# A two-layer hybrid convolution trunk on eight cores: trimmed halo, loads in another order, first groups by halves with filler matmuls, last LayerNorms by halves

## The chip, the cores and the metric

The kernel runs on the 8 cores of one Trainium2 chip. Each core computes 2048 tokens of its own, and no core waits for another. The metric is the device time of the slowest core in microseconds (us), as the median of several runs.

## What is computed

The reference runs two layers (DEPTH = 2) over x of shape (2, 8192, 1024) in float32. Each layer has one input projection, three causal mixers side by side, one output projection and a LayerNorm over the sum with the input:

```python
def hybrid_layer(x, ...):
    h = einsum("btd,de->bte", x, w_in)                       # 1024 -> 4608
    a_bg, a_cg, a_v, a_z, b_v, b_g, b_z, c_u, c_z = split(h) # 9 parts of 512
    y_a = a_bg * conv3(a_cg * a_v) * silu(a_z)               # A: short conv
    u_b = silu(layer_norm(conv31(b_v * sigmoid(b_g))))       # B: conv over 31
    y_b = u_b * silu(b_z)
    p = trailing_mean(c_u, windows 2, 4, 8, 16) - c_u        # C: pooling
    y_c = (p @ pool_w + pool_b) * pool_scale * silu(c_z)
    out = concat(y_a, y_b, y_c) @ w_out                      # 1536 -> 1024
    return layer_norm(ALPHA * x + out, ln_g, ln_b)
```

A token needs earlier tokens: 2 in mixer A, 30 in mixer B and 15 in mixer C, in each layer.

## The kernel before

**Tokens.** A core holds its 2048 tokens and 64 before them, the halo (`HALO = 64`, `TOK = 2112`). The halo is computed again on each core, so that no core needs another's first layer. The work is cut into four units (`UNITS`, L475 and after): layer 0 block 0, layer 0 block 1, layer 1 block 0, layer 1 block 1. `unit_tiles` cuts a unit into tiles of tokens: in block 0 three tiles, (0, 320), (320, 384), (704, 384) in layer 0 and (32, 288), (320, 384), (704, 384) in layer 1; in block 1 two tiles of 512. The later tiles get what lies before them from small tail buffers.

**Groups.** The input projection is computed with channels on the partitions. `group` (L509) makes one 128-channel output of one tile: 8 matmuls (L523) that add up over the 1024 inputs into one PSUM bank, with as many columns as the tile has tokens. Steps are made of groups: `B_step` has three (value `v`, gate `g`, `z`), `A_step` four (`v`, `cg`, `z`, `bg`), `C_step` two (`u`, `z`). Each kind has four channel groups, so a unit has 36 groups per tile. `unit_order` puts them in order: in unit 0 B0, A0, B1, B2, B3, A1, A2, A3, C0 to C3; in the others all B, all A, all C.

**Mixer B.** Inside `B_step`, `glu` makes the gated values (ScalarE, then VectorE) and issues four small DMAs from SBUF to SBUF on SyncE's queue (L640, in the trace `mem<-mem`), which lay out shifted copies. `conv` (L670) then runs 32 matmuls with 32 output columns of the array each, four side by side; they need `Lm`, which VectorE makes by `emit_diag` (L576) from `dmask` and `w4`. `lnb` and `gate` finish mixer B.

**Loads.** Weights of the input projection (`wrg`, 256 KB on the chip each, one per group) go through a ring of `NSLOT = 9` buffers: `issue_w(k + 9)` follows the last tile that used slot k. They, the transposed input `xT` (five tiles, L497) and `wo` (L491) are issued on GpSimd's queue. The inputs of the residual (`Rb`, five buffers), `lnbc`, `par`, `w4` and the `mem<-mem` copies go through SyncE's queue. At the start GpSimd issues w0, xT tile 0 in two halves of its contraction, w1, w2, xT tile 1, w3, xT tile 2, w4 to w8; SyncE issues six small loads at once.

**Output projection.** `p2_chunk` (L976) takes 128 tokens: twice 12 matmuls of 512 columns, then on VectorE residual and statistics (`res`), a square root on ScalarE, and the scaling. The chunks of a unit are mixed into the B groups of the next one (`p2fill`); those of the last unit come at the end. There all but the last chunk are scaled on ScalarE (L549), multiplied on GpSimd (L553) and shifted on VectorE (L553); the last one is scaled and shifted by halves on VectorE (L558) and stored by halves (L1002).

**Order.** All of it is recorded by `P.add` in program order per engine. A planner (`Clock`, with costs and landing times per instruction) decides at build time where the pieces of the side work stand; `spawn(t, ...)` places something at the planner's time t. A `Res` is the unit of dependence: an `Rb` buffer has one for all of its 1024 columns.

## Time and profile before

| | us |
|---|---|
| median of 3 runs (839.61 to 840.76) | 840.51 |
| the profiled execution | 837.62 |
| its span on the slowest core (core 6) | 836.1 |
| spans of the eight cores | 827.0 to 836.1 |
| TensorE busy (matmuls) | 791.8 |
| VectorE, ScalarE, GpSimd busy | 535.5, 399.7, 298.0 |

The profile is one execution, seen on its slowest core. Busy time of PE is modelled (a matmul's row is longer than the distance to the next one), so the distance from start to start is the better measure of a matmul. PEclk is the TensorE clock that was granted, as a share of 2.4 GHz. The KB of a DMA are those that arrive in SBUF (bf16); in memory weights and xT are float32.

### The profile page before, as it was taken

The page shows a single profiled execution, that of the slowest core. Times are in us where ns is not written, and L with a number is a line of the kernel's source. Part 1 is how long each engine was busy: PE and PEld are TensorE (multiplying, and loading weights), DVE is VectorE, ACT ScalarE, POOL GpSimd, SP SyncE. Part 2 cuts the span into 40 slices and gives each one's busy share as a digit, 9 for nine tenths or more (in the row PEclk, how much of TensorE's full clock was granted, in tenths as well). Part 3 has the DMA queues.
Part 4 walks back from the last instruction along what each step waited for, and adds up shares of the span by engine and source line. Part 5 has one row for each costly group of instructions (what it writes and reads, how often), then busy time and mean ns, then how long its engine had stood idle before and what let it go on. Part 6 is the DMA issues. An engine that isn't in the chain of part 4 may idle for free.

```text
span 836.1 us, 16279 instructions; the slowest of 8 cores (827.0 to 836.1 us)
## 1 busy us (share of the span) xinstructions
PE 791.8 (95%) x5208; PEld 408.6 (49%) x5208; DVE 535.5 (64%) x816; ACT 399.7 (48%) x648; POOL 298.0 (36%) x374
## 2 busy tenths in 40 slices
PE   2999889999999999999999999999999999999993
PEld 1555446654444444445555556666444444444441
DVE  1332148887656568668665567868765565888686
ACT  0222257445646487334555578534543348544421
POOL 3122117737110016336510125653711113772342
PEclk9899989999999999999999999999999999999997
DMA  8969996752565755555555676894266756341042
GB/s 127 204 102 206 164 211 98 114 82 42 143 161 141 188 131 92 86 76 77 128 121 158 172 173 146 139 148 66 39 169 169 189 135 152 58 55 35 1 176 102
DMA packets 59170, 104.01 MB, mean 124 GB/s; under 512 B 7216, under 2 KB 28208, under 8 KB 58576
## 3 DMA queue, kind: packets, MB, share of 16 engines
q0 software_dynamic: 28944, 61.26, 43.4%
q1 hardware_dynamic: 30144, 41.72, 16.7%
q8 instruction: 44, 0.72, 0.4%
q14 instruction: 38, 0.31, 0.1%
HBM read 116.52 MB, written 16.78 MB: 159 GB/s over the span
## 4 chain that ended last, share of the span: by engine, by line
PE 78%; DMA 8%; DVE 8%; issue 3%; SPq 1%; ACT 1%; POOL 0%; DVEq 0%; ACTq 0%; POOLq 0%
PE ps L523 49%; PE ps L976 20%; PE ps L670 7%; DMA mem<-mem 6%; DVE mem L553 5%; DMA xT<-xint 2%; DVE mem L558 2%; PE pT L1060 1%; ACT mem L549 1%; SPq L640 1%; PE ps L700 1%; PE ps L714 1%; PE ps L901 1%; DVE Rb L558 1%; DMA out<-Rb 0%
## 5 line engine op out<-in xcount | busy, mean ns | idle before, releaser
L523 PE MATMUL ps<-xT,wrg 128*128 128x512 bf16 (+3 forms) x2880 | 541.7, 344 | 18.4 <-DMA xT<-xint 15.6
L523 PEld LDWEIGHTS ps<-xT,wrg 128*128 128x128 bf16 x2880 | 279.3, 99 | 258.4 <-issue 38.9
L549 ACT ACTIVATE mem<-ps 128x512 f32<-128x512 f32 (+8 forms) x284 | 132.0, 487 | 148.5 <-PE ps L523 115.1
L976 PE MATMUL ps<-wo,yb 128*128 128x512 bf16 (+1 forms) x792 | 184.3, 379 | 0.5 <-ACT mem L549 0.5
L553 POOL TENSOR_TENSOR yb<-mem 128x512 bf16<-128x512 f32 (+3 forms) x120 | 129.1, 1082 | 137.0 <-ACT mem L549 81.7
L487 POOL DMA_DIRECT2D wrg<-w_in_r x144 | 80.0, 559 | 241.0 <-PE ps L523 154.3
L549 ACT ACT_TABLE_LOAD x72 | 92.4, 1283 | 80.6 <-DVE mv L1011 49.6
L976 PEld LDWEIGHTS ps<-wo,yb 128*128 128x128 bf16 (+1 forms) x792 | 77.2, 98 | 90.7 <-issue 3.2
L553 DVE TENSOR_TENSOR mem<-mem 128x512 f32<-128x512 f32 (+11 forms) x140 | 108.9, 784 | 15.7 <-POOL mem L553 4.0
L549 ACT ACTIVATE mem<-mem,par 128x384 f32<-128x384 f32 (+3 forms) x80 | 57.7, 734 | 87.0 <-DVE mem L553 74.5
L558 DVE SCALAR_TENSOR_TENSOR Rb<-Rb,ps 128x512 f32<-128x512 f32 (+1 forms) x66 | 45.1, 684 | 72.6 <-PE ps L976 72.3
L558 DVE SCALAR_TENSOR_TENSOR mem<-mem,par 128x384 f32<-128x384 f32 (+3 forms) x80 | 67.7, 846 | 15.1 <-ACT mem L549 10.0
L670 PE MATMUL ps<-mem,Lm 128*32 128x384 bf16 (+3 forms) x1280 | 69.2, 349 | 8.1 <-DMA mem<-mem 7.9
L553 DVE TENSOR_TENSOR mem<-ps,mem 128x512 f32<-128x512 f32 (+3 forms) x80 | 46.2, 585 | 42.9 <-PE ps L523 24.8
L558 DVE SCALAR_TENSOR_TENSOR Rb<-Rb,mv,lnbc_s 128x1024 f32<-128x1024 f32 (+2 forms) x54 | 67.9, 1258 | 8.1 <-DMA out<-Rb 2.4
L558 DVE SCALAR_TENSOR_TENSOR mem<-mem,ps 128x384 bf16<-128x384 f32 (+3 forms) x40 | 23.4, 585 | 67.6 <-ACT mem L549 67.6
L670 PEld LDWEIGHTS ps<-mem,Lm 128*32 128x32 bf16 x1280 | 32.9, 98 | 41.8 <-issue 24.4
L990 DVE BATCH_NORM_STATS2 stt<-Rb 128x6 f32<-128x512 f32 (+1 forms) x66 | 45.8, 694 | 6.8
L549 ACT ACTIVATE mem<-ps,par 128x384 bf16<-128x384 f32 (+3 forms) x40 | 24.3, 608 | 51.0 <-PE ps L670 51.0
L553 POOL TENSOR_TENSOR mem<-mem 128x384 f32<-128x384 bf16 (+3 forms) x40 | 42.5, 1072 | 0.3
L558 DVE SCALAR_TENSOR_TENSOR mem<-mem 128x384 bf16<-128x384 f32 (+3 forms) x40 | 34.1, 854 | 6.1 <-DVE mem L553 3.3
L1051 POOL DMA_DIRECT2D x1s<-Rb x16 | 8.7, 542 | 78.5 <-DVE Rb L558 78.5
(48 smaller groups left out, 329.4 us busy)
## 6 DMA issues: line engine op xcount, KB each, us to landing
wrg<-w_in_r POOLq DMA_DIRECT2D x144, 256.0 KB, 5.2
mem<-mem SPq DMA_DIRECT2D x64, 135.0 KB, 3.2
Rb<-xin SPq DMA_DIRECT2D x16, 512.0 KB, 5.3
x1s<-Rb POOLq DMA_DIRECT2D x16, 512.0 KB, 3.8
Rb<-x1s SPq DMA_DIRECT2D x16, 512.0 KB, 4.6
mem<-mem SPq DMA_DIRECT2D x64, 103.0 KB, 5.7
wo<-w_out_r POOLq DMA_DIRECT2D x24, 256.0 KB, 7.4
out<-Rb POOLq DMA_DIRECT2D x8, 512.0 KB, 4.0
```

What stands on the lines that cost most here:

```text
L487: P.add("pool", lambda e: e.dma_start(out=wrg_t[:, k % NSLOT].rearrange("p k c -> p (k c)"), in_=w_in_d[li, ci]), writes=[R_wrg[k % NSLOT] ...
L523: o = P.add("pe", lambda e, kk=kk: e.matmul(bk.ap[:, 0:N], lhsT=wrg_t[:, s, kk, :], rhs=xT(kk, tok0, N), start=(kk == 0), stop=(kk == 7)), ...
L549: return P.add("act", lambda e: e.activation(out=out, in_=in_, func=func, **kw), reads=reads, writes=writes, cost=cost).fin
L553: return P.add(eng, lambda e: e.tensor_tensor(out=out, in0=in0, in1=in1, op=op), reads=reads, writes=writes, cost=0.15 + n * (0.0022 if en ...
L558: return P.add("dve", lambda e: e.scalar_tensor_tensor(out=out, in0=in0, scalar=scalar, in1=in1, op0=op0, op1=op1), reads=reads, writes=wr ...
L640: o = P.add("sp", lambda e, src=src, s4=s4: e.dma_start(out=Uv[:, s4, :], in_=src), reads=ub.res, writes=[Ub.res[s4]], dma=True, cost=0.7, ...
L670: o = P.add("pe", lambda e, j=j, s4=s4: e.matmul(Pc.ap[32 * s4:32 * s4 + 32, 0:N], lhsT=Lm_t[:, q % 2, s4, j, :], rhs=Uv[:, s4, 4 * j:4 * ...
L700: o = P.add("pe", lambda e: e.matmul(Pq.ap[:, 0:N], lhsT=ones_t[:], rhs=sqb[g].ap, start=(g == 0), stop=(g == 3)), reads=[R_ones] + sqb[g] ...
L714: o = P.add("pe", lambda e, g=g: e.matmul(Ps.ap[:, 0:N], lhsT=ones_t[:], rhs=cbs[g].ap, start=(g == 0), stop=(g == 3)), reads=[R_ones] + c ...
L976: o = P.add("pe", lambda e: e.matmul(Po.ap[0:n, :], lhsT=yb_t[:, ec, off:off + n], rhs=wo_t[:, ec, h * 512:(h + 1) * 512], start=(idx == 0 ...
L990: return P.add("dve", lambda e: e.bn_stats(out=st_t[0:n, pp, h, :], in_=Rt[:, h * 512:(h + 1) * 512]), reads=[Rr], writes=[R_st[pp]], cost ...
L1051: fst = P.add("pool", lambda e: e.dma_start(out=x1_d[xi], in_=Rt), reads=[Rr], writes=[R_x1[xi]], dma=True, cost=0.6, land=1.8).fin
```

## The change

It has these parts.

1. **Halo.** Tile 0 of block 0 begins 32 tokens later, (32, 288) in layer 0 and (64, 256) in layer 1. `reach` gives the groups whose output is looked back on their extra columns: 32 for B `v` and `g`, 2 for A `v` and `cg`, 16 for C `u`. The loads of xT and the chunks stay.
2. **First loads.** GpSimd issues w0, xT tile 0 first half, w1, its second half, w2, w3, xT tile 1 in two halves, w4 to w6, xT tile 2, w7, w8. SyncE's first loads wait for w0; `w4` and `par` of layer 1 and `idb` move to `late_loads`, and so does `corr`, a chain of small VectorE operations.
3. **First groups by halves.** `halves` writes several groups side by side, first the matmuls of contraction blocks 0 to 3 of each, then 4 to 7. After tile 1 come A0 of tiles 0 and 1, then B0 and A0 of tile 2. `keep_warm` puts matmuls of 128 columns on a zeroed tile before them, as many as fill the planner's waiting time. A Tanh on one element makes ScalarE load its table at the start.
4. **Later loads.** `late_loads` moves from the planner's 60 to 100, xT tiles 3 and 4 from 70 and 90 to 140 and 160, the first `Rb` loads from 100 to 165 and after. In unit 0 no `wo` is loaded in A0 and A1, two per tile in A2 and A3. Landing costs of the planner are higher.
5. **End.** An `Rb` buffer has one `Res` per 512 columns. The residuals of the last three chunks go into the memory of `xT`, loaded during the last unit's A groups. The last but one chunk is multiplied and shifted by halves, one of the four half operations on VectorE and three on GpSimd.

```diff
     if li == 0:
-        return [(0, 320), (320, 384), (704, 384)]
-    return [(32, 288), (320, 384), (704, 384)]
+        return [(32, 288), (320, 384), (704, 384)]
+    return [(64, 256), (320, 384), (704, 384)]
+
+def reach(li, blk, t, back):
+    a, n = unit_tiles(li, blk)[t]
+    d = back if blk == 0 and t == 0 else 0
+    return a - d, n + d, d
...
-        R_Rb = mk("Rb", NRB)
+        R_Rb = [mk("Rb%d_" % i, 2) for i in range(NRB)]
...
+        def keep_warm(until):
+            n = int((until - 0.4 - now()) / 0.055)
+            for _ in range(max(0, n)):
+                P.add("pe", lambda e: e.matmul(banks[6].ap[:, 0:128], lhsT=yb_t[:, 0, 0:128], rhs=yb_t[:, 0, 0:128], start=True, stop=True),
+                      reads=[R_y[0][b] for b in range(4)], writes=banks[6].res, cost=0.0554)
+
+        def halves(u, jobs):
+            bks = [main_bank(1) for _ in jobs]
+            for h in range(2):
+                for bk, (ci, tok0, N) in zip(bks, jobs):
+                    s = win[(u, ci)] % NSLOT
+                    xb = list(blocks(tok0, N))
+                    keep_warm(P.ready_at([R_wrg[s]] + [R_xT[b][4 * h] for b in xb]))
+                    for kk in range(4 * h, 4 * h + 4):
+                        o = P.add("pe", lambda e, kk=kk, bk=bk, s=s, tok0=tok0, N=N: e.matmul(
+                            bk.ap[:, 0:N], lhsT=wrg_t[:, s, kk, :], rhs=xT(kk, tok0, N), start=(kk == 0), stop=(kk == 7)),
...
-            Pv, _ = group(u, 3 * g, tok0, N, last)
+            i0, M, d = reach(li, blk, t, 32)
+            Pv, _ = group(u, 3 * g, i0, M, last)
...
-                spawn(max(f + LAG, o.fin + 1.0), conv(u, g, t, off, N, Ub, Uv, last))
+                spawn(max(f + LAG + (4.0 if u == 0 else 0.0), o.fin + 1.0), conv(u, g, t, off, N, d, Ub, Uv, last))
...
+        FREE_XT = len(chunks) - 3
+        def home(s):
+            if s < FREE_XT:
+                return Rb_t[:, s % NRB, :], R_Rb[s % NRB]
+            i = s - FREE_XT
+            return xT_t[:, 2048 * i:2048 * i + 2048].bitcast(F32), R_far[i]
...
-            def store(eng, src, dst):
-                o = P.add(eng, lambda e: e.dma_start(out=dst, in_=src), reads=[Rr], dma=True, cost=0.6, land=1.8)
+            def store(eng, c):
+                o = P.add(eng, lambda e: e.dma_start(out=out_d[xi][:, c], in_=Rt[:, c]), reads=rr(c), dma=True, cost=0.6, land=1.8)
...
+                    if s == len(chunks) - 2:
+                        a, b = slice(0, 512), slice(512, 1024)
+                        f = tt("dve", Rt[:, b], Rt[:, b], lnbc_t[0:n, 0, b], ALU.mult, [Rr[1], R_lnbc], [Rr[1]])
+                        f = max(f, tt("pool", Rt[:, a], Rt[:, a], lnbc_t[0:n, 0, a], ALU.mult, [Rr[0], R_lnbc], [Rr[0]]))
+                        yield f
+                        tt("pool", Rt[:, b], Rt[:, b], lnbc_t[0:n, 1, b], ALU.add, [Rr[1], R_lnbc], [Rr[1]])
+                        f = tt("pool", Rt[:, a], Rt[:, a], lnbc_t[0:n, 1, a], ALU.add, [Rr[0], R_lnbc], [Rr[0]])
...
+        P.add("dve", lambda e: e.memset(yb_t[:, 0, 0:512], 0.0), writes=[R_y[0][b] for b in range(16)], cost=0.1)
+        P.add("pool", lambda e: e.memset(eps_t[:], LN_EPS), writes=[R_eps])
+        act(sd_t[:, 0, 0:1], eps_t[:], AF.Tanh, [R_eps], [R_sd[0]])
         issue_w(0)
         load_xT(0, 0, 4)
+        issue_w(1)
         load_xT(0, 4, 8)
-        issue_w(1)
         issue_w(2)
-        load_xT(1, 0, 8)
         issue_w(3)
+        load_xT(1, 0, 4)
+        load_xT(1, 4, 8)
+        for k in range(4, 7):
+            issue_w(k)
         load_xT(2, 0, 8)
-        for k in range(4, NSLOT):
+        for k in range(7, NSLOT):
             issue_w(k)
-        spload(dm_t[:], dmask_d, [R_dm])
+        spload(dm_t[:], dmask_d, [R_dm], [R_wrg[0]])
...
             spload(lnbc_t[:].rearrange("p a d -> p (a d)"), lnbc_d[0], [R_lnbc])
-        spawn(26.0, call(corr))
-        spawn(60.0, call(late_loads))
-        spawn(70.0, call(lambda: load_xT(3, 0, 8)))
-        spawn(90.0, call(lambda: load_xT(4, 0, 8)))
+            spload(w4_t[:, 1, :], w4_d[1], [R_w4[1]])
+            spload(par_t[:, 1].rearrange("p g c -> p (g c)"), par_d[1], [R_par[1]])
...
+            corr()
+        spawn(100.0, call(late_loads))
+        spawn(140.0, call(lambda: load_xT(3, 0, 8)))
+        spawn(160.0, call(lambda: load_xT(4, 0, 8)))
         for s in range(NRB):
-            spawn(100.0 + 4 * s, call(lambda s=s: load_Rb(s)))
+            spawn(165.0 + 5 * s, call(lambda s=s: load_Rb(s)))
```

TensorE's queue at the start of unit 0, before (`ps` is a PSUM bank, L523 a group's matmuls, L670 a convolution):

```order
L193 UNCONDITIONAL_BRANCH
L523 MATMUL ps<-xT,wrg 128x320 x24
L523 MATMUL ps<-xT,wrg 128x384 x48
L523 MATMUL ps<-xT,wrg 128x320 x8
L670 MATMUL ps<-mem,Lm 32x320 x32
L523 MATMUL ps<-xT,wrg 128x320 x24
L670 MATMUL ps<-mem,Lm 32x384 x32
L523 MATMUL ps<-xT,wrg 128x384 x24
L670 MATMUL ps<-mem,Lm 32x384 x32
L523 MATMUL ps<-xT,wrg 128x384 x40
```

Three groups of tile 0 came first, then all of B0. The same place now (L521 are the fillers, L532 the groups by halves, L551 the other groups):

```order
L521 MATMUL ps<-yb 128x128 x112
L532 MATMUL ps<-xT,wrg 128x320 x4
L521 MATMUL ps<-yb 128x128 x10
L532 MATMUL ps<-xT,wrg 128x320 x4
L521 MATMUL ps<-yb 128x128 x23
L532 MATMUL ps<-xT,wrg 128x320 x8
L532 MATMUL ps<-xT,wrg 128x288 x8
L521 MATMUL ps<-yb 128x128 x2
L532 MATMUL ps<-xT,wrg 128x290 x8
L521 MATMUL ps<-yb 128x128 x24
L532 MATMUL ps<-xT,wrg 128x384 x32
L551 MATMUL ps<-xT,wrg 128x290 x8
```

There are 171 fillers, and A0's first group has moved into the waits for xT.

VectorE's queue at the very end, from the statistics of the last chunk on, before (Rb is the last two chunks' data):

```order
L1011 BN_AGGR mv<-stt 128x2
L558 SCALAR_TENSOR_TENSOR Rb<-Rb,mv,lnbc_s 128x512
L553 TENSOR_TENSOR Rb<-Rb,lnbc_s 128x1024
L1021 RECIPROCAL mv<-sdt 128x1
L558 SCALAR_TENSOR_TENSOR Rb<-Rb,mv,lnbc_s 128x512 x3
```

And now:

```order
L1062 BN_AGGR mv<-stt 128x2
L581 TENSOR_TENSOR xT<-xT,lnbc_s 128x512
L586 SCALAR_TENSOR_TENSOR xT<-xT,mv,lnbc_s 128x512
L1072 RECIPROCAL mv<-sdt 128x1
L586 SCALAR_TENSOR_TENSOR xT<-xT,mv,lnbc_s 128x512 x3
```

The shift of the last but one chunk over 1024 columns has left VectorE; a multiplication over 512 has come.

## Rows read from the trace of the kernel before

**Rows 1.** The page, parts 1 and 2: busy time, and TensorE's clock by slices

```profile
PE 791.8 (95%) x5208; PEld 408.6 (49%) x5208; DVE 535.5 (64%) x816; ACT 399.7 (48%) x648; POOL 298.0 (36%) x374
...
PEclk9899989999999999999999999999999999999997
```

**Rows 2.** Stretches, core 6: length, busy per engine, PEclk, DMA share, GB/s

```profile
core 6: us, PE busy (x) PEld busy (x) DVE busy (x) ACT busy (x) POOL busy (x), PEclk, DMA share, GB/s
...
21.70:31.20 9.50, 9.50 (x41) 4.88 (x42) 0.73 (x2) 0.98 (x2) 0.68 (x2) 0.69 1.06 187
...
90.00:95.00 5.00, 2.65 (x15) 1.21 (x13) 0.55 (x1) 0.54 (x2) 1.06 (x2) 1.00 0.95 232
95.00:100.00 5.00, 4.84 (x40) 2.48 (x41) 1.40 (x2) 0.64 (x2) 0.00 (x0) 0.66 0.89 162
...
110.00:115.00 5.00, 3.25 (x21) 1.66 (x18) 2.02 (x4) 4.77 (x9) 2.88 (x4) 1.00 0.99 178
115.00:120.00 5.00, 2.75 (x30) 1.30 (x30) 1.85 (x3) 0.04 (x1) 0.00 (x0) 0.63 1.02 275
120.00:125.00 5.00, 5.00 (x22) 2.54 (x22) 3.00 (x5) 2.53 (x4) 0.00 (x0) 0.69 0.60 237
130.00:200.00 70.00, 68.21 (x427) 41.10 (x425) 62.83 (x97) 35.62 (x78) 44.55 (x57) 1.00 0.61 95
```

**Rows 3.** Timeline of PE, start to 22 us: start, length, what, idle before

```profile
11.64 1.23 PE L523 MATMUL ps<-xT,wrg 128*128 128x320 bf16 x4 [11.64 <-DMA xT<-xint]
13.83 1.23 PE L523 MATMUL ps<-xT,wrg 128*128 128x320 bf16 x4 [0.96 <-DMA xT<-xint]
15.38 3.26 PE L523 MATMUL ps<-xT,wrg 128*128 128x320 bf16 x16 [0.32 <-DMA wrg<-w_in_r]
21.68 0.80 PE L523 MATMUL ps<-xT,wrg 128*128 128x384 bf16 x2 [3.04 <-DMA xT<-xint]
```

**Rows 4.** The chain of waits, pieces: start, length, what

```profile
34.65 11.46 DMA mem<-mem
...
47.70 12.30 PE ps L523 x79
...
82.29 12.73 DMA mem<-mem
...
103.28 14.15 DMA mem<-mem
...
325.84 46.62 PE ps L523 x216
```

**Rows 5.** Timeline of POOL, 75 to 108 us: issue of xT tiles 3 and 4

```profile
81.90 0.54 POOL L497 DMA_DIRECT2D xT<-xint  x1
...
102.73 0.55 POOL L497 DMA_DIRECT2D xT<-xint  x1
```

**Rows 6.** DMA issues, first 60, 60 to 77, 100 to 120 us: count, KB, landing

```profile
par<-params SPq DMA_DIRECT2D x2, 18.0 KB, 9.1
...
mem<-mem SPq DMA_DIRECT2D x12, 103.0 KB, 5.5
lnbc_s<-lnbc SPq DMA_DIRECT2D x1, 1024.0 KB, 7.7
...
xT<-xint POOLq DMA_DIRECT2D x1, 1024.0 KB, 14.4
```

**Rows 7.** Timeline of DVE and ACT, first 22 us

```profile
4.70 2.36 DVE L576 TENSOR_TENSOR Lm<-dmask_s,w4s 128x1024 bf16<-128x1024 f32 x2 [4.70 <-DMA w4s<-w]
...
17.64 1.28 ACT L549 ACT_TABLE_LOAD   x1 [17.64 <-PE ps L523]
```

**Rows 8.** Timeline of POOL and DVE, the last 13 us

```profile
823.39 2.34 POOL L553 TENSOR_TENSOR Rb<-Rb,lnbc_s 128x1024 f32<-128x1024 f32 x1 [2.83 <-ACT Rb L549]
...
824.87 1.42 DVE L558 SCALAR_TENSOR_TENSOR Rb<-Rb,mv,lnbc_s 128x512 f32<-128x512 f32 x1
826.21 1.21 DVE L553 TENSOR_TENSOR Rb<-Rb,lnbc_s 128x1024 f32<-128x1024 f32 x1
827.34 0.15 DVE L1021 RECIPROCAL mv<-sdt 128x1 f32<-128x1 f32 x1
827.61 0.75 DVE L558 SCALAR_TENSOR_TENSOR Rb<-Rb,mv,lnbc_s 128x512 f32<-128x512 f32 x1
830.77 1.60 DVE L558 SCALAR_TENSOR_TENSOR Rb<-Rb,mv,lnbc_s 128x512 f32<-128x512 f32 x2 [2.41 <-DMA out<-Rb]
```

159 lines of the change are left out of this document (99 added, 60 removed).

## The prediction

> **What bounds the kernel now.** I read the page first: matmuls fill 95% of the span and no other engine passes 64% [rows 1]. So TensorE (PE) is the bound, and the time is the PE work at full rate plus what PE loses. The full rate comes from the longest unbroken piece of the chain of waits: 216 matmuls of 512 columns in 46.62 us, 215.8 ns each [rows 4], which is 512 columns at 2.4 GHz plus 2.5 ns. By that rule 384 columns cost 162 ns, 320 cost 136 and 288 cost 122. Then I looked for the losses, in the clock by slices and in the stretches. They lie in three places; between 130 us and the last matmul PE is nearly dense (68.21 of 70 us even in the mixer stages of unit 0 [rows 2]).
>
> *The start.* Nothing runs before 11.64 us; then PE waits 0.96, 0.32 and 3.04 us for transfers [rows 3]. After that wait the granted clock falls: it averages 0.69 from 21.7 to 31.2 us [rows 2], so 2 x 0.31 x 9.5 = 5.9 us run at 1.2 GHz, which costs 2.9 us. The third convolution of B0 ends at 47.70 and 40 matmuls of A0 follow [rows 4], as the order above shows, so B0 and A0 are done at 47.70 + 40 x 0.162 = 54.2 us.
>
> *Two holes in the B stage.* From 90 to 100 us PE is idle 2.35 + 0.16 us, from 110 to 120 us 1.75 + 2.25 us: 6.5 us. The clock shows 0.66, 0.63 and 0.69 in the stretches from 95, 115 and 120 [rows 2]: half of the 3.4 us at 1.2 GHz in the first is lost, at most half of PE's 2.75 busy us in the second, half of 3.1 us in the third, 4.6 us. Together 11.2 us. The chain shows why: both times PE waits for the mem<-mem copies of a convolution, which take 12.73 and 14.15 us to land [rows 4] where the median before is 5.5 [rows 6]. They are issued 0.4 and 0.5 us behind xT tiles 3 and 4 (81.90 and 102.73 [rows 5]), 1024 KB each.
>
> *The tail.* VectorE (DVE) works alone after the last matmul. Its scaling of the first half takes 1.42 us beside a GpSimd instruction (0.75 without one), it shifts the other chunk for 1.21 us, and the second half waits 2.41 us for the store of the first [rows 8], because both halves are one resource.
>
> **The change, part by part.** The sum is made against the profiled execution, 837.6 us with a span of 836.1; the median of the runs is 2.9 us above it.
>
> *Halo.* Per unit of block 0, columns that go: 16 groups lose 32 (all z, bg), 8 lose 30, 4 lose 16, B's v and g nothing: 816 columns, 8 matmuls each, 6528 columns, 2.72 us at 2.4 GHz. The convolutions lose 4 x 8 x 32 columns (four matmuls run side by side), 0.43 us, the statistics and the pool map 384 columns, 0.16. Twice 3.3 is 6.6 us. ACT, DVE and GpSimd work shrinks too. In unit 0's later stages DVE is busy 62.83 of 70 us [rows 2], so a little may not reach the end: I take 6.3 (4.5 to 6.6).
>
> *Start.* The rows give the transfer rate: the second half of xT tile 0 (320 KB) comes 2.19 us after the first, w1 (256 KB) 1.55 us later, and w2 with xT tile 1 (1024 KB) 6.30 us later [rows 3]. In the new order, from 11.6: w1 13.2, second half 15.3, w2 16.9, w3 18.4, halves of tile 1 20.7 and 23.0, w4 to w6 24.6, 26.1, 27.7, xT tile 2 32.4. The first sixteen matmuls of 384 columns run on the first half, 20.7 to 23.3, the other sixteen end at 25.9. Then come 24 small ones (2.9 us), 80 of 384 columns (13.0) and three convolutions (3.6), none of them before its transfer: 45.4 us. New waits stand against that. SyncE's small loads now wait for w0, perhaps until 9 us, and such a load took 9.1 us to land among the others [rows 6]; DVE's two Lm products (2.36 us [rows 7]) need them and stand ahead of the first gated values, which are then ready at about 20 instead of 17 us. The earlier table load gives back 1.28 us of that [rows 7]. The copies still share the engines with the big loads (11.46 us for the third set [rows 4]). I charge 3.0 us for three convolutions (0 to 7). So 48.4 instead of 54.2; 0.6 of this is the halo, 5.2 is new (1 to 8).
>
> The 112 fillers before the first data cost nothing if they end before 11.6: at 2.4 GHz they need 112 x 0.056 = 6.3 us, at 1.2 GHz throughout 11.9. If they begin at 1.2 us (an assumption; the trace has no early PE work), they end between 7.5 and 13.1; I expect them to be through before the data, as part of them runs fast. The other 59 (3.3 us) fill waits that the rows above show longer. What they are to give is that the real matmuls run at 2.4 GHz. If they fail, the 16 last ones cost 2.6 us more; that is in the bound.
>
> The split of tile 1 gives 2.6 us of this term: whole, its 32 matmuls would begin at 23.0. The two halves of tile 0 landed 2.19 us apart [rows 3], and four matmuls used the time between. The Trainium skill (DMA: Bandwidth & Descriptors, "Rules for kernel authors") says of two transfers to disjoint partition halves not to bother, as they serialize over the same engines. These halves are of the contraction, not of the partitions, and serializing is what lets the first be used early; by the rule the term would be 2.6 us, not 5.2.
>
> *Holes.* xT tiles 3 and 4 now stand in GpSimd's queue between weights of the C groups, where no copies are in flight; `lnbc` and the first `Rb` loads follow the last copies of B3 on SyncE's queue. Only the weights, three or four at a time, are left beside copies, and then copies took 5.5 us [rows 6], less than the planner's lag of 10. I take the whole 11.2 us (7 to 13; more than 11.2, as short waits at other convolutions may go too).
>
> *What the moves may cost.* The DMA share from 130 to 200 us was 0.61 [rows 2]; 43 busy us there get two xT tiles and three wo more, some 18 us by the rate above, in about 65: full, but not over. xT tile 4 is issued when the third C group is done. Its user, the second tile of unit 1, comes 14.6 us of PE work behind it: six groups of C (7.2 us), three groups of 512 columns (5.2) and ten single matmuls (2.2). It landed in 14.4 us at worst [rows 6]. I charge 0.3 us (0 to 4). In `late_loads` DVE must wait for `par` of layer 1, behind `lnbc` (7.7 us [rows 6]) on SyncE; DVE has 27 instructions between its last copy's source and that place, some 15 us by the durations of their kinds. I charge 0.6 us (0 to 5); behind it stand the PSUM reads that free banks for PE.
>
> *Tail.* The 2.41 us wait goes. DVE does 0.6 us of multiplication for the last but one chunk instead of 1.21 us of shift: counted from 824.87, 0.6 + 0.75 + 0.3 + 3 x 0.8 makes 828.9 instead of 832.4, if GpSimd disturbs nothing, a gain of 3.4. But three half operations of GpSimd, 1.17 us each by half of 2.34 [rows 8], now lie beside these. The 1.42 against 0.75 us [rows 8] shows that one disturbs the other. If each pair ran strictly one after the other, DVE would end near 831.0, a gain of 1.4. I take 2.2 (0.5 to 3.4). The Trainium skill (SBUF — State Buffer, "Who interferes with whom") has the strict form: a VectorE instruction with two SBUF inputs and a GpSimd one that reads SBUF take turns as wholes. By it the term would be 1.4 and the time 0.8 us more.
>
> *Sum.* 6.3 + 5.2 + 11.2 + 2.2 - 0.3 - 0.6 = 24.0 us. The profiled execution would take 813.6 us, the median **816.5**.
>
> **Rivals.**
> - *The copies stay late.* If it is the weights and not xT that hold them back, the 11.2 us stay: 827.7. For it: the copies of B0 took 11.46 us without xT 3 and 4 [rows 4]. Against: then the start's loads were in flight, and the holes follow both xT issues at once. 0.08.
> - *A new wait on DVE.* The small loads at the start or `par` come late and DVE blocks the queue in front of PSUM reads: up to 5 us more, 821.5. For it: both waits are new. 0.07.
> - *The halo does not pay in unit 0,* because DVE sets the pace there: half of the term lost, 819.7. Against: PE is 97% busy there. 0.05.
> - *Slower: xT tile 4 starves unit 1.* The transfers of 70 to 120 us are now pushed into the time of twelve wo and eight weights. From 14.6 us after its issue each us of landing is a us of PE idle. To eat the gain of 24 it must land after 39 us. With all twelve wo (3072 KB), four weights (1024 KB) and both tiles (2048 KB) still queued, that is 6 x 6.3 = 38 us and about 2 to arrive: 25 us late, and some 2 us for the half clock that follows, 843.5. Against: wo is issued 25 us and more before it, and queues drain meanwhile. 0.03.
>
> **How the numbers follow.** The forecast as worked out has 0.77, and its own bounds added up in part give 811 to 823. The range must take in the first two rivals' centres in part: 810.5 to 826.5; beyond lie the late copies, the slower case and a little of the top of each bound, some 0.15 in all. A measurement of this kernel tells 0.2% (1.7 us) from no change. Only the last rival ends above that: slower 0.03, the same 0.01, faster 0.96.
>
> **What would show it.** Right: the first real matmul near 11 us with a clock of 1.0, and none below it until 60 us; B0 and A0 done near 48 us; no stretch of 5 us between 60 and 130 us with PE below 4.5; the last scaling on DVE without a wait for the store; PE work 3.3 us smaller in each unit of block 0. Wrong: copies that land after 10 us in the B stage, DVE waiting for par or w4, PE waiting for xT near the start of unit 1, or matmuls at 1.2 GHz behind the fillers.

## The result, and the profile after

The changed kernel takes 829.24 us (median of 4 runs, 828.67 to 829.31), the kernel before beside it 840.36 (839.61 to 840.76): a ratio of 0.987 [0.985, 0.988], 11.1 us less. Forecast were 816.5 us and 24 less; the range began at 810.5 and ended at 826.5, so the time lies above it. (Disturbed executions are left out of all comparisons here.) The profiled execution took 828.67 us, with spans of 822.9 to 827.1 us over the cores.

The page of the changed kernel, parts 1, 2 and 5 (a group: busy us, mean ns | idle before it, and what ended most of it), against [rows 1]:

```profile
PE 785.5 (95%) x5323; PEld 418.2 (51%) x5379; DVE 526.0 (64%) x817; ACT 398.5 (48%) x649; POOL 299.7 (36%) x377
...
PEclk9999999999999999999999999999999999999997
...
L551 PE MATMUL ps<-xT,wrg 128*128 128x512 bf16 (+7 forms) x2786 | 516.5, 339 | 12.2 <-ACT mem L577 9.9
...
L699 PE MATMUL ps<-mem,Lm 128*32 128x384 bf16 (+3 forms) x1280 | 65.2, 343 | 4.7 <-DMA mem<-mem 3.7
```

In the page's slices the clock no longer dips; a slice is 20.7 us long, and two short dips at the start don't show in it (below). PE's idle time in front of the groups has a new owner: ScalarE, 9.9 of 12.2 us, whose instructions at L577 read the PSUM banks and so free them. Stretches on core 6, columns as in [rows 2]:

```profile
90.00:95.00 5.00, 5.00 (x56) 2.91 (x54) 0.73 (x3) 1.48 (x3) 1.55 (x3) 1.00 0.73 128
95.00:100.00 5.00, 5.00 (x64) 3.69 (x60) 2.89 (x6) 1.91 (x4) 0.03 (x1) 1.00 0.86 123
110.00:115.00 5.00, 5.00 (x50) 2.90 (x43) 3.71 (x4) 3.51 (x8) 4.78 (x7) 1.00 0.76 123
115.00:120.00 5.00, 4.22 (x30) 2.74 (x29) 3.84 (x17) 2.36 (x6) 3.56 (x7) 1.00 0.70 91
120.00:130.00 10.00, 9.21 (x60) 5.80 (x61) 3.41 (x10) 9.19 (x14) 3.97 (x6) 1.00 1.04 155
130.00:200.00 70.00, 62.16 (x376) 35.72 (x376) 63.15 (x94) 33.78 (x76) 47.82 (x61) 1.00 0.82 120
```

The holes of 90 to 120 us are gone, but for 0.8 us in the last stretch. In their place PE is busy 62.16 of 70 us from 130 on, where it was 68.21 [rows 2]. The trace names ScalarE as the releaser of most of these waits, but ScalarE is busy for only 33.78 of the 70 us and VectorE for 63.15; that the waits go back to VectorE is what the experiments below show. And from 120 to 130 us VectorE lies idle for 6.6 us beside a full ScalarE.

To see where time comes and goes I take, from each trace, when the weights of the n-th projection group are loaded on PE (fillers left out), as a mean over the eight cores, and subtract the same for the kernel before:

| before group | 21 | 36 | 54 | 72 | 96 | 108 (unit 1) | 216 | 288 (unit 3) | last matmul | end |
|---|---|---|---|---|---|---|---|---|---|---|
| changed minus before, us | -2.7 | -3.0 | -14.5 | -11.0 | -6.9 | -5.7 | -7.1 | -10.1 | -10.4 | -8.4 |

(Unit 2 begins at group 180.) The lead of 14.5 us that closed holes and start had earned is cut to 5.7 inside unit 0, behind the holes. The last 2 us go at the very end.

The start, PE on core 6, against [rows 3] (start, length, what, idle before):

```profile
1.87 8.76 PE L521 MATMUL ps<-yb 128*128 128x128 bf16 x112 [1.87 <-DVE yb L1141]
10.55 0.70 PE L532 MATMUL ps<-xT,wrg 128*128 128x320 bf16 x4
...
16.49 3.69 PE L532 MATMUL ps<-xT,wrg 128*128 128x320 bf16 x16 [2.32 <-DMA xT<-xint]
...
22.66 5.36 PE L532 MATMUL ps<-xT,wrg 128*128 128x384 bf16 x32
27.86 5.71 PE L551 MATMUL ps<-xT,wrg 128*128 128x290 bf16 x40
33.50 0.30 PE L699 MATMUL ps<-mem,Lm 128*32 128x288 bf16 x1
34.88 0.28 PE L699 MATMUL ps<-mem,Lm 128*32 128x288 bf16 x1 [1.08 <-DMA mem<-mem]
36.41 0.28 PE L699 MATMUL ps<-mem,Lm 128*32 128x288 bf16 x1 [1.25 <-DMA mem<-mem]
38.01 2.08 PE L699 MATMUL ps<-mem,Lm 128*32 128x288 bf16 x29 [1.32 <-DMA mem<-mem]
```

The projection starts early and on this core without a pause at tile 1, then the first convolution waits 3.7 us for its copies. The second half of tile 0's xT, forecast for 15.3, is used at 16.49. Behind both waits (2.32 us for xT, 3.7 us for the copies) the granted clock is halved for 3.4 us, from 17.1 and from 37.5 us:

```profile
16.40:20.20 3.80, 3.71 (x19) 2.42 (x20) 1.88 (x2) 0.44 (x1) 0.00 (x0) 0.59 1.06 162
37.50:41.00 3.50, 2.99 (x33) 1.72 (x34) 0.00 (x0) 0.50 (x1) 0.00 (x0) 0.51 0.03 10
```

So sixteen matmuls of 320 columns take 3.69 us, where at 135 ns each, as those from 10.55 us on, they take 2.2. In the traces of all cores seven of eight have a dip to 1.2 GHz that begins between 31 and 38 us, and none has one between 60 and 130 us, where the kernel before has one on every core.

The tail, POOL and DVE on core 6, against [rows 8]:

```profile
814.13 0.75 DVE L586 SCALAR_TENSOR_TENSOR xT<-xT,mv,lnbc_s 128x512 f32<-128x512 f32 x1
814.36 3.30 POOL L581 TENSOR_TENSOR xT<-xT,lnbc_s 128x512 f32<-128x512 f32 x2 [0.82 <-DVE xT L581]
814.98 0.16 DVE L1072 RECIPROCAL mv<-sdt 128x1 f32<-128x1 f32 x1
815.26 3.81 DVE L586 SCALAR_TENSOR_TENSOR xT<-xT,mv,lnbc_s 128x512 f32<-128x512 f32 x3
```

The wait for the store is gone, but VectorE's three last operations take 3.81 us where three single ones take 2.3. SyncE, which waits for the stores, is through at 822.6, yet the span ends at 827.1. The trace has one more record: GpSimd's DRAIN at the end of the block, which ends at 826.89, 9.2 us after GpSimd's last operation (817.67). On core 6 before the change it ends 9.15 us after the last operation (825.74), at 834.9, just under SyncE's end of 835.9. There it cost nothing.

### The profile page after: what moved, and what is told of

Its sections match the earlier page's. It is cut to its first block, busy times and chain, and to the rows that moved or that the text cites. A ratio compares the mean times of both kernels' runs of the same rounds, so it can differ in the third digit from the quotient of the medians.

```text
span 827.1 us, 16537 instructions; the slowest of 8 cores (822.9 to 827.1 us)
## 1 busy us (share of the span) xinstructions
PE 785.5 (95%) x5323; PEld 418.2 (51%) x5379; DVE 526.0 (64%) x817; ACT 398.5 (48%) x649; POOL 299.7 (36%) x377
## 4 chain that ended last, share of the span: by engine, by line
PE 80%; DVE 8%; DMA 5%; issue 4%; ACT 1%; SPq 1%; DVEq 0%; POOL 0%; ACTq 0%; POOLq 0%
PE ps L551 50%; PE ps L1024 20%; PE ps L699 7%; DVE mem L581 4%; DMA mem<-mem 3%; DVE mem L586 1%; DMA w4s<-w 1%; PE pT L1122 1%; ACT mem L577 1%; PE ps L743 1%; PE ps L729 1%; DVE xT L586 1%; PE ps L932 1%; DVE mem L763 1%; DMA wrg<-w_in_r 1%
## 5 line engine op out<-in xcount | busy, mean ns | idle before, releaser
L551 PE MATMUL ps<-xT,wrg 128*128 128x512 bf16 (+7 forms) x2786 | 516.5, 339 | 12.2 <-ACT mem L577 9.9
L551 PEld LDWEIGHTS ps<-xT,wrg 128*128 128x128 bf16 x2816 | 271.3, 98 | 238.3 <-issue 25.6
L577 ACT ACTIVATE mem<-ps 128x512 f32<-128x512 f32 (+13 forms) x284 | 131.3, 485 | 170.4 <-PE ps L551 103.1
L1024 PE MATMUL ps<-wo,yb 128*128 128x512 bf16 (+1 forms) x766 | 180.7, 379 | 1.3
L577 ACT ACTIVATE mem<-mem,par 128x384 f32<-128x384 f32 (+3 forms) x80 | 57.5, 729 | 78.1 <-DVE mem L581 66.0
L586 DVE SCALAR_TENSOR_TENSOR Rb<-Rb,ps 128x512 f32<-128x512 f32 (+1 forms) x60 | 41.0, 684 | 70.3 <-PE ps L1024 70.2
L581 DVE TENSOR_TENSOR mem<-ps,mem 128x384 f32<-128x384 f32 (+5 forms) x80 | 45.7, 577 | 50.5 <-PE ps L551 28.8
L699 PE MATMUL ps<-mem,Lm 128*32 128x384 bf16 (+3 forms) x1280 | 65.2, 343 | 4.7 <-DMA mem<-mem 3.7
L586 DVE SCALAR_TENSOR_TENSOR Rb<-Rb,mv,lnbc_s 128x1024 f32<-128x1024 f32 (+1 forms) x50 | 64.3, 1285 | 5.0 <-DVE mv L1072 0.3
L1038 DVE BATCH_NORM_STATS2 stt<-Rb 128x6 f32<-128x512 f32 (+1 forms) x60 | 41.6, 694 | 6.2
L577 ACT ACTIVATE mem<-ps,par 128x384 bf16<-128x384 f32 (+3 forms) x40 | 24.1, 603 | 44.2 <-PE ps L699 44.0
L604 DVE TENSOR_TENSOR Lm<-dmask_s,w4s 128x1024 bf16<-128x1024 f32 x16 | 20.0, 1254 | 27.5 <-DMA w4s<-w 16.6
```

What stands on the lines that cost most here:

```text
L551: o = P.add("pe", lambda e, kk=kk: e.matmul(bk.ap[:, 0:N], lhsT=wrg_t[:, s, kk, :], rhs=xT(kk, tok0, N), start=(kk == 0), stop=(kk == 7)), ...
L577: return P.add("act", lambda e: e.activation(out=out, in_=in_, func=func, **kw), reads=reads, writes=writes, cost=cost).fin
L581: return P.add(eng, lambda e: e.tensor_tensor(out=out, in0=in0, in1=in1, op=op), reads=reads, writes=writes, cost=0.15 + n * (0.0022 if en ...
L586: return P.add("dve", lambda e: e.scalar_tensor_tensor(out=out, in0=in0, scalar=scalar, in1=in1, op0=op0, op1=op1), reads=reads, writes=wr ...
L604: P.add("dve", lambda e: e.tensor_tensor(out=Lm_t[:, q % 2].rearrange("p s j c -> p (s j) c"), in0=dm_t[:].unsqueeze(1).to_broadcast([128, ...
L699: o = P.add("pe", lambda e, j=j, s4=s4: e.matmul(Pc.ap[32 * s4:32 * s4 + 32, 0:N], lhsT=Lm_t[:, q % 2, s4, j, :], rhs=Uv[:, s4, d + 4 * j: ...
```

## The experiments

They ran later, in five series. In these the medians of the kernel before are 833.9 to 835.8 us, and the changed kernel, run again unedited in one of them, took 827.4 and 827.5. So its gain is 7.1 us there against 11.1; where the kernel before gained its 5 us is not settled. Ratios are to the kernel before of the same series; two times from different series can differ by the 2 us between these medians. The ratios of after_again and e4 are from two executions and from one, and so have no interval. "LN" is the time at which the weights of mixer B's LayerNorm statistics in unit 0 are first loaded on PE, "unit 1" that of its first group, both as means over the cores; "tail" is from the last weight load on PE to the end. The trace of the kernel before is that of the first occasion. Four traces have the same code up to unit 1 (the changed kernel, after_again, e6, e15); in them unit 1 starts at 184.2 to 185.3 us, so a difference under 1 us in that column says nothing.

The expectations name theories by letters. V: from about 120 us on the amount of VectorE's work sets the pace. K: the moved corr chain holds the stage back. D: the transfers moved there do. L and S: the time counts at which mixer B's last convolutions and statistics are done. W: `w4` lands too late. G: GpSimd's last instruction ends the span.

| run | ratio | gain, us of 835 | LN | unit 1 | tail |
|---|---|---|---|---|---|
| kernel before (first trace) | 1 | | 103.1 | 191.0 | 14.3 |
| after_again | 0.9915 | 7.1 | 100.8 | 184.5 | 16.3 |
| e1_halo | 0.9891 [0.9874, 0.9907] | 9.1 | 104.5 | 185.2 | 14.1 |
| e2_moves | 0.9880 [0.9866, 0.9895] | 10.0 | 98.0 | 180.3 | 14.2 |
| e9_halo_moves | 0.9852 [0.9830, 0.9875] | 12.4 | 96.2 | 178.7 | 14.1 |
| e14_cut_e9 | 0.9805 [0.9787, 0.9824] | 16.3 | 95.6 | 175.0 | 14.4 |
| e3_cut_after | 0.9895 [0.9871, 0.9919] | 8.8 | 100.5 | 180.3 | 16.4 |
| e5_cut_before | 0.9994 [0.9983, 1.0005] | 0.5 | 103.1 | 189.3 | 14.3 |
| e4_corr_early | 0.9934 | 5.5 | 102.2 | 182.6 | 16.4 |
| e10_corr_late | 0.9847 [0.9830, 0.9864] | 12.8 | 96.0 | 180.5 | 14.4 |
| e11_lag_back | 0.9962 [0.9950, 0.9974] | 3.2 | 102.0 | 186.5 | 16.3 |
| e12_lag_corr | 0.9910 [0.9889, 0.9931] | 7.5 | 102.3 | 182.8 | 16.4 |
| e13_lag_first | 0.9876 [0.9851, 0.9900] | 10.4 | 95.7 | 178.8 | 16.3 |
| e7_small_now | 0.9911 [0.9896, 0.9927] | 7.4 | 99.0 | 182.9 | 16.4 |
| e8_nofill | 0.9940 [0.9920, 0.9961] | 5.0 | 99.7 | 183.4 | 16.4 |
| e6_tail_dve | 0.9884 [0.9863, 0.9905] | 9.7 | 100.4 | 184.2 | 12.2 |
| e15_tail_old | 0.9879 [0.9864, 0.9895] | 10.1 | 100.4 | 184.2 | 13.3 |
| e16_all | 0.9811 [0.9787, 0.9836] | 15.8 | 95.1 | 177.4 | 12.2 |
| e17_all_nofill | 0.9791 [0.9776, 0.9805] | 17.5 | 94.5 | 176.6 | 12.1 |

**Halo and later loads, each alone and together.** e1 is the kernel before with the halo hunks of the diff, e2 with this, e9 with both:

```diff
-        spawn(60.0, call(late_loads))
-        spawn(70.0, call(lambda: load_xT(3, 0, 8)))
-        spawn(90.0, call(lambda: load_xT(4, 0, 8)))
+        spawn(100.0, call(late_loads))
+        spawn(140.0, call(lambda: load_xT(3, 0, 8)))
+        spawn(160.0, call(lambda: load_xT(4, 0, 8)))
...
-            spawn(100.0 + 4 * s, call(lambda s=s: load_Rb(s)))
+            spawn(165.0 + 5 * s, call(lambda s=s: load_Rb(s)))
```

and two `wo` per tile in A2 and A3 of unit 0. (e9 also has the changed kernel's `load_Rb`, which keeps the `Rb` loads in order when they are asked for out of it.)

> The kernel before with the trimmed halo alone (part 1 of the change). The prediction's term: 6.3 us less than before, 834.1 where before is 840.4. Theory V (from about 120 us to the end of unit 0 the elementwise work of VectorE and ScalarE sets the pace once TensorE has not lost time earlier; here TensorE still loses the holes of the B stage, so unit 0 gains little from fewer TensorE columns, and unit 2 gains 1.5 to 3 us, as the trace of the changed kernel shows 1.8): 3 to 5 us, 835.4 to 837.4.

> The kernel before with the later loads alone (the times of late_loads, xT tiles 3 and 4, the first Rb and the wo loads of unit 0). corr, the small loads, the planner's costs and the order of groups stay. The prediction's term: 11.2 us less, 829.2, since the two holes between 90 and 120 us close. Theory V: the holes close all the same (TensorE at least 4.5 us busy in each 5 us between 90 and 115 us, lead of 8 to 12 us over before at 120 us), but VectorE, busy over 90 per cent from 125 us on, lets TensorE wait there and takes back 4 to 8 us: 833 to 837. Theory D (it is the transfers moved behind 130 us that slow the end of unit 0): the same time, but TensorE or GpSimd waits there for DMA and VectorE is idle for more than 15 per cent.

> The kernel before with the trimmed halo and the later loads, nothing else. Alone they gave 8.9 and 9.8 us against 835.95. Theory K: they add up, 17 to 19 us less than before, and the lead of TensorE at the start of unit 1 is 15 us or more, so the rest of the change costs 6 to 8 us. Theory V: VectorE lets TensorE lead by no more than some 11 us at the start of unit 1; 12 to 14 us less than before.

e1 gains more than either theory said, e2 what the prediction had for the holes, so theory V in its first form (the lead of the holes is taken back by itself) is wrong: e2 leads by 10.5 us at group 54 and still by 10.8 at unit 1. But 9.1 and 10.0 give 12.4 together, as theory V had it for e9 (12 to 14; theory K 17 to 19). At group 54 the leads are 4.3, 10.5 and 12.6 us: the halo alone had closed the second hole (e1, core 6: PE busy 10.00 of 10 us from 110 on), so 2.2 us are counted twice. At unit 1 they are 5.9, 10.8 and 12.3: 2.2 more are missing, behind the holes. In the time 6.7 are missing, each gain being uncertain by 1 to 2 us; the 2.3 that remain are not placed.

**VectorE's share.** One tap of mixer A's convolution left out in channel groups 1 to 3 of unit 0 (nine VectorE instructions, estimated at 4.7 us in the expectation of e3; the result lacks that tap), in the changed kernel (e3), in the kernel before (e5) and in e9 (e14):

```diff
-                for k in (1, 2):
+                for k in ((1,) if u == 0 and g > 0 else (1, 2)):
```

> The changed kernel without one of the two VectorE taps of mixer A's convolution in unit 0, groups 1 to 3: nine instructions of 0.45 to 0.6 us, some 4.7 us of VectorE in the stage from 120 us on; TensorE, ScalarE, GpSimd and the transfers have the same work. It leaves out the tap of the current token in those three channel groups of block 0 of layer 0. Theory V: the time falls by most of that, 3.5 to 5.5 us, from 829.2 to 823.7 to 825.7. Theory D: no more than 0.5 us, 828.7 to 829.2.

> The kernel before without the same nine VectorE taps (it leaves out the same part). Theory V: before the change VectorE had a reserve there, since TensorE came 12 to 15 us later through its holes: at most 1.5 us less, 838.9 to 840.4. If the stage was bound by VectorE as much before the change, it gains the same 3.5 to 5.5 us as in the changed kernel, and the lost lead needs another cause.

> The kernel e9 (before, trimmed halo, later loads) without the nine VectorE taps that e3 and e5 leave out (the tap of the current token in mixer A's convolution, channel groups 1 to 3 of layer 0 block 0). Halo and later loads brought 5.9 and 10.8 us of lead at the start of unit 1 by themselves, 12.3 together. Theory S (VectorE's work takes the missing 4.4 us): the start of unit 1 comes 3.5 to 4.7 us earlier than in e9. The same cut gave 4.2 us there in the changed kernel (e3) and 1.8 in the kernel before (e5). Rival (transfers or ScalarE take them): 0 to 2 us.

Unit 1 starts 4.2 us earlier in e3, 1.8 in e5 and 3.8 in e14. So VectorE's work there is paid nearly in full once the holes are closed, and less than half before; the 1.8 is the weakest of the three, as the cores of the kernel before start unit 1 anywhere from 187.6 to 193.5 us, but its time agrees (0.5 us less, -0.4 to 1.4). In e14 the time falls by 4 us as well. In e3 it does not show: 828.4 and 826.4 beside 827.4. Of its 4.2 us 2.2 are lost between groups 108 and 120; the last matmul still comes 2.3 us earlier as a mean over the cores, but the slowest core lies 4 us above the mean of the eight. The same work, taken from VectorE in the same place, thus shows in PE's calendar in both kernels, but in the time clearly in one. e9 from 110 us on, core 6, against the rows of the changed kernel above:

```profile
110.00:120.00 10.00, 10.00 (x72) 6.75 (x70) 9.69 (x14) 8.38 (x15) 8.81 (x15) 1.00 0.67 85
120.00:130.00 10.00, 10.00 (x63) 6.06 (x62) 9.66 (x15) 7.29 (x11) 9.70 (x13) 1.00 1.07 161
130.00:180.00 50.00, 46.51 (x302) 28.79 (x301) 41.54 (x72) 22.11 (x57) 28.04 (x39) 1.00 0.87 136
```

VectorE is full from 110 us on and has no gap until 130; the changed kernel's has one. The DMA share is 1.07 and 0.87 in the last two stretches, yet none of PE's 3.5 us of waits from 130 to 180 us is for a transfer (all are for VectorE and ScalarE), which speaks against theory D.

**The moved corr chain.** e4 takes it back to 26 us in the changed kernel, and loads `w4` and `par` of layer 1 with the first small loads; e10 moves the chain to 100 us in e9. The edit of e4, in part:

```diff
-            corr()
+        spawn(26.0, call(corr))
```

> The changed kernel, but corr at the planner's 26 us as before, and w4 and par of layer 1 loaded with the first small loads. Theory K (the moved chain of fourteen small VectorE instructions, 114.2 to 118.8 us, holds back ScalarE's work behind it; ScalarE then sets the pace from 120 to 130 us and VectorE lies idle there for over 6 us): 4 to 7 us less than the changed kernel. Theory V (VectorE's total of work from 110 us on sets the pace wherever the chain stands): the chain still leaves the stage, so 3 to 4.5 us less. Theory D (the transfers moved there): no change.

> The kernel e9 (before, trimmed halo, later loads) with corr moved from the planner's 26 to 100 us, as the change does it. Theory K: 4 to 7 us slower than e9. Theory V: 3 to 4.5 us slower, or nothing where VectorE has a reserve. Theory D: the same as e9.

> The changed kernel once more, unedited, as the yardstick on the chip of these runs: 0.9867 of the kernel before.

In the changed kernel the chain stands here, behind the Lm product (DVE, core 6; its first and last rows, ten like them between):

```profile
111.19 1.95 DVE L763 RECIPROCAL mem<-mem 128x288 f32<-128x288 f32 x1 [2.01 <-ACT mem L577]
113.06 1.21 DVE L604 TENSOR_TENSOR Lm<-dmask_s,w4s 128x1024 bf16<-128x1024 f32 x1
114.19 0.70 DVE L1169 TENSOR_SCALAR cnt<-aux_s 128x16 f32<-128x16 f32 x1
...
118.49 0.17 DVE L1172 TENSOR_SCALAR corr<-cnt 128x16 f32<-128x16 f32 x1
118.58 0.23 DVE L1175 TENSOR_TENSOR bsc<-par 128x4 f32<-128x4 f32 x2
118.74 0.46 DVE L581 TENSOR_TENSOR mem<-mem 128x288 f32<-128x288 f32 x1
```

It holds VectorE for 4.4 us. Without it (e4) the gap at 120 us shrinks (VectorE busy 7.02 of 10 us, where it was 3.41). The way from LN to unit 1 is 3.3 us shorter in e4 than in the changed kernel, and 2.0 longer in e10 than in e9; but LN comes 1.4 us later in e4, so that unit 1 gains 1.9 and 1.8 us. That is neither the 4 to 7 of theory K nor the 3 to 4.5 of theory V, and nothing of it reaches the time: e9 and e10 agree within their intervals, and e4, a single execution, loses its share again by group 120. Theory K falls. For the times of this pair theory D, which had no change, was right, though no wait for a transfer bears it out.

**The lag of the convolutions.** e11 undoes the extra 4 us, e12 undoes corr too, e13 keeps them for channel group 0 alone.

```diff
-                spawn(max(f + LAG + (4.0 if u == 0 else 0.0), o.fin + 1.0), conv(...))
+                spawn(max(f + LAG + (4.0 if u == g == 0 else 0.0), o.fin + 1.0), conv(...))
```

> The changed kernel with the planner's lag of the convolutions of unit 0 at 10 us again instead of 14. Theory L (the 4 us of lag move the last convolutions of mixer B, and with them the LayerNorm statistics, 4 us later; VectorE, which is idle between 80 and 110 us and busy nine tenths from there on, starts its pile of work later and ends it later): the first table load for the square root near 103 instead of 107 to 109 us, the lead of TensorE at the start of unit 1 3 to 4.5 us larger, the time 3 to 5 us less than the changed kernel's 827.4. Against it: the convolutions may wait for their copies again; then holes of 1 us and more show between 60 and 110 us, and the gain is 0 to 2 us. Theory V alone (only the amount of VectorE's work counts): no change.

> The same, and corr, w4 and par of layer 1 early as before the change (e11 and e4 together). By theory L with the 1.9 us that corr early gave at the start of unit 1: 4.5 to 7 us less than the changed kernel, 820.5 to 823; the start of unit 1 may take 1 to 2 us of it back by a wait for xT tile 4.

> The changed kernel with the extra 4 us of lag for the convolutions of channel group 0 alone; the others go back to 10 us. e11 took the 4 us from all of them, and the very first convolution then stopped TensorE for 7 us. Theory S (the start of unit 1 follows the time at which the first convolution of B3, and behind it the LayerNorm statistics, is done, by 84 to 88 us, since VectorE is the bound of all that follows them in unit 0: 93.5 and 178.7 us in e9, 96.8 and 184.5 in the changed kernel, 99.2 and 182.8 in e12): the start as in the changed kernel, the first convolution of B3 at 92 to 94 us, the start of unit 1 at 179 to 182 us, and 2.5 to 5 us less than the changed kernel's 827.4. Rival (only how early TensorE is counts, and the lag costs nothing): no change, and new short waits for copies.

e11 is 4 us slower than the changed kernel, where theory L had it 3 to 5 faster. The lag has a use, at the first convolution, which PE now meets too early (e11, core 6):

```profile
30.02 0.28 PE L699 MATMUL ps<-mem,Lm 128*32 128x288 bf16 x1 [2.01 <-DMA mem<-mem]
32.62 0.40 PE L699 MATMUL ps<-mem,Lm 128*32 128x288 bf16 x1 [2.33 <-DMA mem<-mem]
34.69 0.40 PE L699 MATMUL ps<-mem,Lm 128*32 128x288 bf16 x1 [1.67 <-DMA mem<-mem]
36.27 2.08 PE L699 MATMUL ps<-mem,Lm 128*32 128x288 bf16 x29 [1.18 <-DMA mem<-mem]
```

e12 stops there too (8.1 us of waits) and gains nothing clear on the changed kernel (826.6 us, expected 820.5 to 823). With the lag kept there and dropped elsewhere (e13), LN comes at 95.7 instead of 100.8 and unit 1 at 178.8 instead of 184.5. The table shows the rule. In all kernels with the trimmed halo and whole work, unit 1 starts 80.4 to 82.5 us behind LN when corr is early and 83.2 to 84.5 when it is late, with a standard deviation over the eight cores of 0.4 us at most, though PE reaches group 54 anywhere from 101.4 to 114.2 us in them. From LN on VectorE (with ScalarE) sets the pace; PE's lead counts only as far as it brings LN forward. The runs e3 and e14 bear that out (LN moves by 0.6 us at most, the way shrinks by 4.0 and 3.2), and e13 (LN moves by 5.1 us, unit 1 by 5.7). The rule is good to 2 us: with corr early, the kernels whose LN comes before 97 us need 82.1 to 82.5 us from there, those with LN after 102 us 80.4 to 80.7.

**Small loads and fillers.**

```diff
-        spload(dm_t[:], dmask_d, [R_dm], [R_wrg[0]])
+        spload(dm_t[:], dmask_d, [R_dm])
...
-            n = int((until - 0.4 - now()) / 0.055)
+            n = 0
```

> The changed kernel with SyncE's first small loads issued at once instead of behind w0; the order of all instructions is the same. Theory W (w4, landed at 18 us behind that wait, holds back Lm, the first gated values and their copies, and the first convolution waits 4 us for them): the convolution's waits of 4.7 us between 33 and 40 us fall to 1 or 2 us, and the first real matmul comes up to 1 us later, since the small loads share the engines with w0. At the end of the kernel 0 to 2 us less, because the lead is given back in unit 0's A and C stages. Rival (the copies wait for the engines that the weights fill): no change of those waits.

> The changed kernel without its 171 filler matmuls. If they do what they are there for, the real matmuls of the first 10 us run at 1.2 GHz and the groups of tile 0 and tile 1 end 2 to 5 us later (g21 at 52 to 55 instead of 50.2 us), and that shifts all that follows, as the 1.7 us of e7 did: 2 to 4 us slower than the changed kernel. If the real matmuls wait for transfers anyway, less than 1 us.

e7: the first convolution waits 2.2 us on core 6 instead of 2.7 (after_again) or 3.7, unit 1 starts 1.7 us earlier and the last matmul 1.4, as theory W has it, since LN moves too; the time falls by 0.6 us, too little to tell from none. e8: PE's first groups without fillers, core 6:

```profile
9.51 2.37 PE L532 MATMUL ps<-xT,wrg 128*128 128x320 bf16 x8 [9.51 <-DMA xT<-xint]
14.24 4.72 PE L532 MATMUL ps<-xT,wrg 128*128 128x320 bf16 x24 [2.36 <-DMA xT<-xint]
20.39 2.76 PE L532 MATMUL ps<-xT,wrg 128*128 128x384 bf16 x16 [1.44 <-DMA xT<-xint]
23.47 2.76 PE L532 MATMUL ps<-xT,wrg 128*128 128x384 bf16 x16 [0.32 <-DMA xT<-xint]
26.06 4.21 PE L551 MATMUL ps<-xT,wrg 128*128 128x290 bf16 x29
```

The first eight matmuls of 320 columns take 2.37 us; most start 267 ns behind one another, the pace of 1.2 GHz, where with fillers it is 135 ns. (The clock view has no record before 17 us in e8, so here the pace has to tell.) So the fillers do raise the clock for the first real matmuls. But it fell again in the changed kernel's next wait of 2.3 us, and in both kernels PE stands waiting for transfers: group 21 starts 1.1 us earlier without fillers (49.1 us, as against 49.8 to 50.9 in the four traces with the same start). The kernel as a whole is 1.6 us slower all the same (829.0 beside 827.4), from 1.0 us lost at the start of unit 1 and 1.3 in the last 22 groups of unit 3, far from the fillers; I can't tie that to them, and e17 speaks against it.

**The tail.** e6 puts all four half operations on VectorE; e15 goes back to full widths and keeps the two resources.

```diff
-                        f = max(f, tt("pool", Rt[:, a], Rt[:, a], lnbc_t[0:n, 0, a], ALU.mult, ...))
+                        f = max(f, tt("dve", Rt[:, a], Rt[:, a], lnbc_t[0:n, 0, a], ALU.mult, ...))
...
-                        tt("pool", Rt[:, b], Rt[:, b], lnbc_t[0:n, 1, b], ALU.add, ...)
-                        f = tt("pool", Rt[:, a], Rt[:, a], lnbc_t[0:n, 1, a], ALU.add, ...)
+                        tt("dve", Rt[:, b], Rt[:, b], lnbc_t[0:n, 1, b], ALU.add, ...)
+                        f = tt("dve", Rt[:, a], Rt[:, a], lnbc_t[0:n, 1, a], ALU.add, ...)
```

> The changed kernel with all four half operations of the last but one chunk on VectorE instead of one. VectorE ends later by three halves of 0.65 us, less what GpSimd no longer disturbs: about 820 us instead of 819.1 on the profile's scale. Theory G (the span ends with GpSimd's last instruction of the block, which ends 9.2 us after GpSimd's last operation, at 817.7 in the changed kernel): GpSimd's last operation is then that of the chunk before, some 3 to 5 us earlier, and the span ends with SyncE's stores, 13 us behind the last matmul instead of 16.3: 3 to 4 us less than the changed kernel. Rival (the end follows VectorE's last operation and the stores): 0.5 to 1 us more.

> The changed kernel with the last but one chunk multiplied over its full width on GpSimd and shifted over its full width on VectorE, as before; the halves of Rb as separate resources stay. Theory G: the wait for the first store is gone, VectorE and SyncE end some 2.4 us earlier than before relative to the last matmul, but GpSimd's last operation stands where it stood, so the span ends 1 us less behind the last matmul than before at most: 13.0 to 14.0 us (before 14.4, the changed kernel 16.3, e6 12.2), 2.3 to 3.3 us less than the changed kernel. Rival (halves on GpSimd are no worse than the full width): the same as the changed kernel within 0.5 us.

Theory G holds in both, with 824.2 and 824.4 us. The end of e6, core 6:

```profile
807.04 2.35 POOL L581 TENSOR_TENSOR xT<-xT,lnbc_s 128x1024 f32<-128x1024 f32 x1 [1.46 <-ACT xT L577]
...
815.05 1.29 DVE L581 TENSOR_TENSOR xT<-xT,lnbc_s 128x512 f32<-128x512 f32 x2
816.25 0.16 DVE L1072 RECIPROCAL mv<-sdt 128x1 f32<-128x1 f32 x1
816.52 2.27 DVE L586 SCALAR_TENSOR_TENSOR xT<-xT,mv,lnbc_s 128x512 f32<-128x512 f32 x3
```

With one engine doing all of it, VectorE ends at 818.8, 7.3 us behind the start of the last residual (811.50); beside GpSimd, by halves, it was 7.2 (811.85 to 819.07), and in e15, with the full width multiplied on GpSimd, 6.9 (809.58 to 816.50). And the span ends with SyncE, 0.2 us behind its last record. In e15 GpSimd's last operation ends at 812.35, SyncE is through at 820.2, GpSimd's DRAIN ends at 821.58, again 9.2 us behind its last operation, and the span at 821.8.

**Put together.** e16 has e13, e7, e4 and e6; e17 drops the fillers too and issues xT tile 4 at 152:

> The changed kernel with what held put together: extra lag for channel group 0 alone (e13, 4.4 us at the last matmul), small loads at once (e7, 1.4 to 1.7), corr, w4 and par of layer 1 early (1.9 at the start of unit 1 in e4 and e10), all four half operations of the tail on VectorE (e6, 4.1 behind the last matmul). If they add up: 9 to 11 us less than the changed kernel's 827.4, 816.5 to 818.5, and so 3.5 to 5.5 us less than e9. If VectorE's work behind the statistics of mixer B takes a part again, as it did of halo and later loads: 819 to 821.

> e16 without the fillers (without them the first real matmul came 0.7 us earlier in e8, and TensorE stayed 1.1 us ahead until unit 1) and with xT tile 4 at the planner's 152 instead of 160 us, since TensorE waited 1.9 us for it in e9 at the start of unit 1. 0.5 to 2 us less than e16 if both hold; the same if the lead is taken back in unit 0.

e16 takes 819.0 us, 8.4 less than the changed kernel: not the full 9 to 11, but the 819 to 821 of the other case, for which the expectation had VectorE take a part again; what takes it was not tried. Its last weight load comes 4.4 us before that of after_again, as e13's does (4.5), and its tail is 4.1 shorter, as e6's is: early small loads and early corr added nothing at the last weight load. e17 takes 817.0, 0.979 [0.978, 0.981] of the kernel before and the best of all. Its unit 1 starts 0.8 us earlier than e16's and its last matmul comes 4.2 us earlier; 1.7 of that arises between groups 216 and 240, and 1.2 in the last 22 groups of unit 3, where some kernels pause and others don't (e8 above). What of it belongs to the fillers and what to tile 4 was not tried apart.

## Why the prediction was wrong

Three steps failed: the addition of the terms, two parts of the change with no price, and the path at the end. On the scale of the experiments the sum should have been 24.0 and is 7.1 (11.1 on the first occasion). Holes and halo together gave 12.4 for the 17.5 of the forecast; all the rest (start, lag, corr, tail) was to give 6.5 and cost 5.3.

**PE's being "nearly dense" from 130 us on was read for the wrong engine.** The 11.2 us of the holes, the halo and the start were added up as if PE were the bound everywhere. I had the row (VectorE 62.83 of 70 us [rows 2]) and used it for a rebate of 0.3 us on the halo. It meant that PE and VectorE were both near their limit there, and that what PE gained in front of this stage counts only as far as it brings LN forward. The measured price at unit 1 is 2.2 us for halo and later loads together (e9), and in the time up to twice that; for the start it is not measured apart from the lag.

**A part with no price.** "LAG + 4" was not costed; the forecast worked with a lag of 10. It moved LN from 96.2 (e9) to 100.8, and undoing it behind group 0 gave 5.7 us at unit 1 and 3.4 in time (e13). **Corr** was called "a chain of small VectorE operations" and costed at nothing, though the charge for `late_loads` was on the same engine: 4.4 us of VectorE, 1.8 to 1.9 at unit 1, nothing measurable in the time. The two fit the path: e9 starts unit 1 12.3 us before the kernel before; 4.6 for LN and 1.3 for the longer way from LN to unit 1 leave 6.4, and after_again has 6.5.

Term by term:
- *Holes, 11.2 (7 to 13):* right, 10.0 [8.8, 11.2] alone. The rival that the copies stay late is out: PE is busy 5.00 of 5.00.
- *Halo, 6.3 (4.5 to 6.6):* 9.1 [7.8, 10.5] alone, where it also shortens the holes; 2.4 on top of the later loads (e9 less e2, uncertain by 1.9 and 1.2 us; at the last weight load the traces have 4.5). The rival "the halo does not pay in unit 0" is nearer than its 0.05.
- *Start, 5.2 (1 to 8), and 0.6 of the halo:* group 21 comes 2.7 us earlier, not 5.8: at 50.9 as a mean, forecast 48.4, where the kernel before had it at 53.6 and not 54.2. Tile 1's last matmul ends at 26.9 as a mean, forecast 25.9. The rest is lost behind it: the first convolution waits 3.7 us on core 6 where 3.0 were charged, and the half clock behind that wait, 3.4 us long and so worth some 1.7 us by estimate, had no price (the forecast had no clock below 1.0 until 60 us). Lm is begun at 18.3 us, since w4 stands behind w0, and the gated values are ready at 21.1, forecast 20; the rival with small loads late was right in kind, and e7 prices it at 1.7.
- *DVE waiting for par, PE for xT tile 4:* neither is seen in the changed kernel. In e9, which is 6 us earlier, PE waits 1.9 us for xT.
- *Tail, 2.2 (0.5 to 3.4):* it lost 2.0. I followed VectorE and the stores to the end and never asked what GpSimd still had to do. VectorE's own end came as forecast: 7.2 us behind the start of the last residual, where it was 9.4 (822.97 to 832.37 [rows 8]).

On the ports: from 814.36 to 819.07 VectorE and GpSimd do together, in 4.7 us, what takes 2.3 us (three operations of VectorE, as in e6) and 2.3 (two of GpSimd by half of 2.34 [rows 8]) alone. That is the strict form, one after the other. The Trainium skill (SBUF — State Buffer, "Who interferes with whom") says so, and the trace agrees. The strict form was my lower price (a gain of 1.4), yet VectorE's end gained 2.2: the first of the three GpSimd operations (812.27, 1.26 us) ran beside the statistics of the last chunk (812.63, 0.69 us as elsewhere), and neither took longer for it; the rest of the difference is not taken apart.

On the halves of a transfer: on core 6 tile 1's 32 matmuls ran without a pause (22.66, 5.36 us), so there its split gave at most what the fillers ahead of it hid. On six of the other cores the 17th starts 3.1 to 3.5 us behind the first, where sixteen take 2.6, so it waited for the second half; in e8 (core 6) it starts 3.1 us behind. The first 16 matmuls used that time. The Trainium skill (DMA: Bandwidth & Descriptors, "Rules for kernel authors") advises against splits by partition; no run here took the split alone away, and its worth stays open.

## What to carry to other kernels

When a stall is closed, ask which engine is next in the stage behind it, and when its pile of work can start: its start, not the bound engine's lead, then sets the time. A lag of 4 us in front of it cost 5 us of its start here; 4.4 us of small instructions inside it lengthened the way by 2 to 3 us. Gains measured one by one do not add where they share a stall or a second bound; a run with a piece of the second engine's work left out shows it, in the times at which later groups start if not in the whole time. At the end of a kernel follow every engine to the last record, those that are not waited for by data too.

## What I had not expected of the hardware

GpSimd's DRAIN at the end of the block ends 9.14 to 9.23 us after its last operation, on all eight cores of all twenty traces. Work on it in the last 9 us costs even when nothing waits for its result. And splitting two-input work by halves between VectorE and GpSimd gave next to nothing: VectorE alone (e6) was done 7.3 us behind the start of the last residual, both together 7.2; the full width of the multiplication on GpSimd, begun while VectorE took statistics (e15), made it 6.9. The clock is the third: on core 6 a wait of 2.3 us and one of 3.7 us were each followed by 3.4 us at half the clock, in spite of 171 fillers ahead of them.
